# A gated decoder layer in split fp32: opening by column halves, moved low parts, loads and reductions, and last weight chunks by token halves

## The reference, cut to what matters

```
xn = rmsnorm(x, norm_mix); proj = xn @ w_in
k, v = rmsnorm(mem) @ w_k, rmsnorm(mem) @ w_v        # 256 memory rows
ya = (a_b * dwconv3(a_c * a_x)) @ w_out_a
yb = silu(layernorm(dwconv31(b_val * sigmoid(b_glu)) + bias)) @ w_out_b
yx = softmax(q @ k.T / 16) @ v @ w_out_x             # samples: cached k, v
h  = x + (sig(g0)*ya + sig(g1)*yb + sig(g2)*yx) @ w_o
h  = h + (silu(hn @ w_ff_gate) * (hn @ w_ff_up)) @ w_ff_down,  hn = rmsnorm(h)
y  = rmsnorm(h)
```

## Time and profile before

| | |
|---|---|
| median of 3 runs | 1111.93 us (1111.69 to 1114.23) |
| the profiled execution | 1113.01 us, span 1111.3 us |
| TensorE busy | 1089.8 us, 98% of the span |
| VectorE, ScalarE, GpSimd busy | 547.3, 490.6, 132.8 us |
| mean granted TensorE clock | 0.993 of full speed |
| first product of kv0, of kv1, first product of the b stage | 10.15, 18.35, 72.37 us |
| end of the last down product | 1097.6 us |
| moved by the DMA engines | 215.85 MB |

### The profile page before, as it was taken

The page is one execution under the profiler, slowest core; times in us unless marked ns, Lnnn a source line. Parts: engine busy times, 40 slices in busy tenths (PEclk is TensorE's granted clock), DMA queues, the critical chain, the costliest instruction groups (busy, mean ns, idle before and its releaser), DMA issues.

```text
span 1111.3 us, 20957 instructions
## 1 busy us (share of the span) xinstructions
PE 1089.8 (98%) x8997; PEld 1082.8 (97%) x8997; DVE 547.3 (49%) x964; ACT 490.6 (44%) x535; POOL 132.8 (12%) x118
## 2 busy tenths in 40 slices
PE   8999999999999999999999999999999999999996
PEld 7999999999999999999999999999999999999996
DVE  5775667888978564784333523343232332300122
ACT  5634343443334433443446645643444443434431
POOL 6561000002200000000000000000000000000000
PEclk9999999999999999999999999999999999999998
DMA  9857876689796777668786788787777777787863
GB/s 306 259 164 190 213 204 158 201 213 306 212 248 154 184 203 175 152 162 185 184 210 169 185 233 211 169 189 189 202 184 188 179 189 184 174 199 180 197 147 115
DMA packets 135416, 215.85 MB, mean 194 GB/s; under 512 B 4742, under 2 KB 122846, under 8 KB 124582
## 3 DMA queue, kind: packets, MB, share of 16 engines
q0 software_dynamic: 11808, 85.99, 38.8%
q1 hardware_dynamic: 98854, 106.99, 29.7%
q10 hardware_dynamic: 24688, 21.90, 6.4%
HBM read 122.34 MB, written 7.54 MB: 117 GB/s over the span
## 4 chain that ended last, share of the span: by engine, by line
PE 84%; DVE 5%; ACT 2%; DMA 2%; issue 1%; ACTq 0%; DVEq 0%
PE acc L1634 54%; PE acc L1650 27%; DVE o_acc L1291 1%; PE acc L1831 1%; DMA k_st<-in_cache_mem_k_dram 1%; DMA w_l<-w_raw 1%; PE acc L1807 1%; DVE ubyb L1128 1%; PE acc L1608 1%; ACT w_h L544 1%; DVE k_st L1202 1%; ACT w_l L547 0%; DVE sg L1439 0%; DVE yA L1342 0%; DVE ubyb L1443 0%
## 5 line engine op out<-in xcount | busy, mean ns | idle before, releaser
L1634 PE MATMUL acc<-big_h,w_h 128*128 128x260 f32 x2016 | 408.5, 284 | 1.3 <-DVE sg L1328 1.2
L1634 PE MATMUL acc<-big_l,w_h 128*128 128x260 f32 x2016 | 405.8, 283 | 0.0
L1634 PEld LDWEIGHTS acc<-big_h,w_h 128*128 128x128 f32 x2016 | 310.9, 189 | 2.0 <-DVE sg L1328 1.4
L1634 PEld LDWEIGHTS acc<-big_l,w_h 128*128 128x128 f32 x2016 | 311.3, 189 | 0.0
L544 ACT ACTIVATE w_h<-w_raw 128x1024 fp32r<-128x1024 f32 x186 | 186.2, 1050 | 179.4 <-DMA w_raw<-in_w_ff_down_dram 59.8
L1650 PE MATMUL acc<-big_h,w_l 128*128 128x260 f32 x2016 | 253.3, 282 | 1.3 <-DMA w_l<-w_raw 1.3
L1650 PEld LDWEIGHTS acc<-big_h,w_l 128*128 128x128 f32 x2016 | 246.8, 188 | 1.7 <-DMA w_l<-w_raw 1.5
L1128 DVE SCALAR_TENSOR_TENSOR ubyb<-ubyb,prm 128x512 f32<-128x512 f32 (+1 forms) x240 | 180.3, 751 | 15.6 <-DVE ubyb L1128 9.9
L528 POOL DMA_DIRECT2D w_l<-w_raw x82 | 70.0, 854 | 899.8 <-ACT w_l L547 888.5
L547 ACT ACTIVATE w_l<-w_raw 128x2048 fp32r<-128x2048 f32 x82 | 156.2, 1905 | 23.9 <-PE acc L1650 23.9
L1634 PE MATMUL acc<-hg_h,w_h 128*128 128x260 f32 x704 | 141.9, 283 | 0.0
(11 more groups left out here) (212 smaller groups left out, 762.6 us busy)
## 6 DMA issues: line engine op xcount, KB each, us to landing
w_l<-w_raw POOLq DMA_DIRECT2D x82, 1024.0 KB, 7.8
w_raw<-in_w_in_dram SPq DMA_DIRECT2D x36, 1024.0 KB, 5.2
w_raw<-in_w_ff_gate_dram SPq DMA_DIRECT2D x11, 1024.0 KB, 5.3
w_raw<-in_w_ff_up_dram SPq DMA_DIRECT2D x11, 1024.0 KB, 5.2
k_st<-in_cache_mem_k_dram ACTq DMA_DIRECT2D x8, 1024.0 KB, 8.8
v_st<-in_cache_mem_v_dram ACTq DMA_DIRECT2D x8, 1024.0 KB, 11.8
w_raw<-in_w_ff_down_dram SPq DMA_DIRECT2D x8, 1024.0 KB, 6.6
w_raw<-in_w_v_dram SPq DMA_DIRECT2D x4, 1024.0 KB, 6.7
```

Of the source, the lines that this page charges most:

```text
L1634: last = M.matmul(out[:, b, 0:HALF], w_h[:, slot, k, cols], xs[:, k_at + k, b * HALF:(b + 1) * HALF], start=start and k == 0 and xs is x[0 ...
```

## The change

Five parts, named by where they act.

1. **Opening.** Gain, high part, low part and the products of kv0 go by halves of 4 blocks, alternating between the two mem tiles, so that the products of one half run while the other is prepared. ScalarE squares the second mem tile later. The low part of weight chunk 0 is subtracted by VectorE (`first_chunk_lo`), and GpSimd starts with chunk 1 after the first root refinement. Ten filling transposes on TensorE before kv0 are gone.
2. **Low part of x one chunk on.** `prep(c)` no longer ends with `norm_lo`; that follows one chunk later. A second buffer `nrm_o` makes room.
3. **cx stage.** `group_max` comes first on VectorE, ahead of convolution steps and tile products; `sample_sum(1)` moves behind the tile work of its pass; the convolution steps are dealt out anew (same 24).
4. **xT loads** are issued after the loads of chunks ob2 and ob3 instead of ob1 and ob2.
5. **End.** The last two weight chunks are taken for tokens 0 to 259 first and then for 260 to 519; rows, squares, mean and root of the first token half (`ya`) are interleaved with the products of the second (`yb`). Chunk 93 joins `SUB`. The order of uses changes from `y2, d3, y3, ms` to `y2, ya, d3, yb`.

```diff
-WARM, FILL = 16, 10
+WARM = 16
-SUB = (*range(C_B + 2), C_CX + 2, C_CX + 4)
+SUB = (*range(C_B + 2), C_CX + 2, C_CX + 4, C_END - 1)
...
-    for name in ("d0", "d1", "y0", "d2", "y1", "y2", "d3", "y3", "ms"):
-        use(name, 1 if name == "ms" else 2)
+    for name in ("d0", "d1", "y0", "d2", "y1", "y2", "ya", "d3", "yb"):
+        use(name, 1 if name in ("ya", "yb") else 2)
...
+    nrm_b = [nrm_t, at("nrm_o", [P, KT, P], f32, o_ub + 4 * D)]
@@ SyncE, ob stage @@
-                if j in (1, 2):
-                    if j == 1:
+                if j >= 2:
+                    if j == 2:
                         sp.wait_ge(acc_done, T["gb"] + 10)
@@ GpSimd @@
+                if c == 0:
+                    continue
                 if c in SUB:
+                    if c == 1:
+                        pool.wait_ge(refined, 5)
+                    elif c == C_END - 1:
+                        pool.wait_ge(d_used, 7)
@@ ScalarE, opening @@
+            def memory_hi(m, h):
+                act.wait_ge(mem_gain, 2 * m + h + 1)
+                ks = slice(h * HK, (h + 1) * HK)
+                nc.scalar.activation(mn[0][:, ks, m * P:(m + 1) * P], (nrm_t, nrm_2)[m][:, ks, :], ACT.Copy) \
+                    .then_inc(mem_hi, 1)
-            squares(1, P)
-            norm_tile(T["mem"], mn[0], slice(0, P), P)
+            for m, h in itertools.product(range(2), range(2)):
+                memory_hi(m, h)
...
-            norm_tile(T["mem"] + 1, mn[0], slice(P, 2 * P), P, nrm_2)
+            squares(1, P)
@@ VectorE, opening @@
+            memory_gain(0, 0)
+            memory_gain(0, 1)
+            memory_gain(1, 0)
+            memory_lo(0, 0)
+            memory_gain(1, 1)
+            V.memset(mx[:, 0:1], 0.0).then_inc(acc_read, 2)
+            memory_lo(1, 0)
+            memory_lo(0, 1)
+            memory_lo(1, 1)
+            first_chunk_lo(0)
             mean_rows(0)
-            for n in range(2):
-                norm_lo(mn, slice(n * P, (n + 1) * P), P, bufs[n])
+            first_chunk_lo(1)
             refine_rows(0)
...
-                    norm_lo(xn, slice(c * P, c * P + rows), rows, nrm_t)
@@ VectorE, loop over kv chunks c @@
+                if c == 0:
+                    mean_rows(1)
                 if c == 2:
+                    norm_lo(0)
+                if c == 6:
+                    norm_lo(4)
+                if 3 <= c < 6:
+                    norm_lo(c - 2)
@@ VectorE, cx stage @@
-            C3 = ((range(0, 5), range(5, 11)), ((), range(11, 13)), (range(13, 15), range(15, 20)), (range(20, 24), ()))
+            C3 = ((range(0, 3), range(3, 7)), ((), range(7, 13)), (range(13, 15), range(15, 20)), (range(20, 24), ()))
-                    sample_sum(it)
+                    if it > 1:
+                        sample_sum(it)
+                else:
+                    group_max()
-                if it == 0:
-                    group_max()
-                if it == 0:
-                    sample_sum(0)
+                if it < 2:
+                    sample_sum(it)
@@ TensorE, kv0 @@
+                    for h, m, n in itertools.product(range(2), range(2), range(2)):
+                        pe.wait_ge(mem_lo if n else mem_hi, 2 * h + m + 1 if n else 2 * m + h + 1)
@@ TensorE, end @@
+            for low in (False, True):
+                for j in range(2):
+                    last_products(C_END - 2, j, 0, *ks[1], low)
+            for j in range(2):
+                last_products(C_END - 1, j, 0, *ks[2], False)
+            for j in range(2):
+                last_products(C_END - 1, j, 0, *ks[2], True).then_inc(d_half, 1)
+            for j in range(2):
+                last_products(C_END - 2, j, 1, *ks[1], False)
+            last_rows(T["ya"], 0, (h_half, 0))
+            last_sums(T["ya"], 0, 2, 8, 6)
+            for j in range(2):
+                last_products(C_END - 2, j, 1, *ks[1], True)
+            for j in range(2):
+                last_products(C_END - 1, j, 1, *ks[2], False)
+                last_products(C_END - 1, j, 1, *ks[2], True).then_inc(acc_done, 1)
+            last_rows(T["yb"], 2, (acc_read, T["d3"]))
+            last_sums(T["yb"], 2, 3, 10, 7)
```

More of the change, by code:

```diff
@@ new lines, in _ @@
+            dve.wait_ge(y_sq, 7)
+            last_sum(0, HALF)
+            last_rows(T["ya"], 0, slice(0, 2))
+            last_scale(0, slice(0, 2))
+            for j in range(2):
+                use = T["d3"] + j
+                done(use)
+                V.tensor_tensor(h_sb[:, 6 + j, HALF:TOK], acc[use % 4][:, 1, 0:HALF], h_sb[:, 6 + j, HALF:TOK],
+                                ALU.add).then_inc(acc_read, 1)
+            dve.wait_ge(y_sq, 9)
+            last_sum(HALF, TOK)
+            last_rows(T["yb"], 2, slice(2, 5))
@@ L1692, in _ @@
                 pe.wait_ge(row_in[n], 16)
-                flip8(T["mem"] + n, stage[n], P)
-            for n in range(FILL):
-                flip(acc[T["kv0"] % 4][:, 0, 0:P], ident[:, :])
+                flip8(T["mem"] + n, stage[n], P, halfway=mem_flip)
             def prep(c):
@@ new lines, in last_products @@
+            def last_products(c, j, b, k0, kn, low):
+                out = acc[(T["d3"] + j) % 4][:, b, 0:HALF]
+                cols, toks = slice(j * P, (j + 1) * P), slice(b * HALF, (b + 1) * HALF)
+                if b == 0 and j == 0 and low:
+                    if c in SUB:
+                        pe.wait_ge(w_sub, subtracted(c))
+                    else:
+                        pe.wait_ge(w_rest[c % 2], turn(c) * 16)
+                for k in range(kn):
+                    if b == 0 and j == 0 and not low and k % HK == 0:
+                        pe.wait_ge(w_hi, 2 * c + k // HK + 1)
+                    if low:
+                        last = M.matmul(out, w_l[:, c % 2, k, cols], mid[0][:, k0 + k, toks], start=False,
+                                        stop=c == C_END - 1 and k == kn - 1)
+                    else:
+                        for xs in mid:
+                            last = M.matmul(out, w_h[:, c % 2, k, cols], xs[:, k0 + k, toks], start=False, stop=False)
+                return last
@@ new lines, in last_rows, with last_sums @@
+            def last_rows(use, t, ready):
+                free(use)
+                for n in (6, 7):
+                    pe.wait_ge(ready[0], ready[1] + n - 5)
+                    for s in range(2):
+                        a = ((n - 6) * 2 + s) * P
+                        flip(acc[use % 4][:, 0, a:a + P], h_sb[:, n, (t + s) * P:(t + s + 1) * P])
+                    if t:
+                        flip(acc[use % 4][0:TS, 1, (n - 6) * P:(n - 5) * P], h_sb[:, n, TP:TOK])
+            def last_sums(use, t, count, squares, sums):
+                pe.wait_ge(y_hs, sums)
+                pe.wait_ge(y_sq, squares)
+                for i in range(count):
+                    rows = P if t + i < 4 else TS
+                    for n, src in enumerate((hs, sgf[:, 1, :])):
+                        last = M.matmul(acc[use % 4][0:rows, 1, 256 + i:257 + i], src[:, (t + i) * P:(t + i) * P + rows],
+                                        ones[:, 0:1], start=n == 0, stop=n == 1)
+                last.then_inc(acc_done, 1)
```

190 lines of the change are left out of this document (116 added, 74 removed).

## The result

The changed kernel takes 1106.96 us (median of 5, 1104.67 to 1107.67); the kernel before, run beside it, 1112.26 (1111.69 to 1114.23). The medians differ by 5.3 us. By the ratio over all their runs, 0.9945 with a 95% interval of 0.9932 to 0.9957, it is 6.1 us faster (4.8 to 7.6) where 10.3 were forecast, and the median is 1.5 us above the range. The profiled execution is the fastest of the five: 1104.67, span 1102.9.

A forecast was written before the change was run, and what follows sets the result against it. TensorE, busy throughout from 630 to 1097.6 us, was taken as the bound. Savings of 4.2 + 3.1 + 1.3 + 1.7 = 10.3 off 1111.93 gave 1101.6 us; likeliest 1099.5 to 1103.5, range 1098.5 to 1105.5.

The forecast's parts named there:

- The xT loads: ob stage: the later xT loads speed ob0's low-part DMA and remove TensorE's wait, saving 1.3 us, between 0 and 1.3.
- the room only at ob2: ob stage: ob2's low-part DMA, even as slow as 10.0 us, lands 3.0 us before TensorE needs it.
- the delay is moved and not removed: ob stage: by round robin xT delays whatever low-part DMA it meets, by 2.2 us, within 3.0 of room.
- The opening: Up to the b stage: VectorE comes earlier, so the b stage starts near 68.2, saving 4.2 us, between 2.0 and 5.8.
- What came back: Opening: VectorE's new waits for k,v products and ScalarE's copies, and blocked low parts, take back about 2.3 us.
- the low bound of 2.0: Opening: with all four low parts blocked by GpSimd, 2.17 us less, so only 2.0 is saved.
- The cx stage: cx stage: waits for `m_rep` and in cx4 go, 1.8 and 1.3 us, saving 3.1, between 1.5 and 3.2.
- The norm of head 0: cx stage, before cx5's second tile: late next, at 302.1 against 302.8, hidden by 0.7; a slip costs what it slips.
- The end: Last pass to the last store: products end later but stores start earlier, saving 1.7 us net, between 0.7 and 3.0.
- the wait of 1.3 for y2's first rows: Last pass: d3's second tile takes y2's accumulator before VectorE has read it, losing 1.3 us.
- What is added between the products: End: four transposes and four narrow products among TensorE's products, 0.5 + 0.4 us, 0.9 in all.
- The clock: Rival, chance 0.13: the clock falls at the opening's end, before the b stage, costing 1.5 us: 1103.1, twice 1104.6.

The follow-up runs named there:

- c4: The kernel before with only the xT loads moved (part 4 alone): 1115.11 us, ratio 1.0015.
- d1: The changed kernel with each xT half held until TensorE has ended the chunk before (ob0, ob1): 1105.18 us, ratio 0.9932.
- d2: c4 with each xT half held until TensorE has ended the chunk before (ob0, ob1): 1112.90 us, ratio 0.9992.
- a4: The changed kernel without part 4, its xT loads in their old places: 1106.47 us, ratio 0.9948.
- c3: The changed kernel with only the 928 KB convolution state copy moved, to the second down pass: 1104.70 us, ratio 0.9922.
- a3: The kernel before with part 5, the end, alone: 1111.30 us, ratio 0.9987.
- a1: The kernel before with part 3, the cx stage, alone: 1109.76 us, ratio 0.9973.
- a2: The kernel before with parts 1 and 2, the opening and the later low part of x, alone: 1111.39 us, ratio 0.9987.
- b2: The changed kernel with xT loaded in quarters behind the loads of ob2, ob3, wo0 and wo1: 1104.87 us, ratio 0.9925.
- b4: The changed kernel with squares, root and refinement of x tiles 2 to 4 put behind prep(1): 1104.14 us, ratio 0.9929.
- b1: The changed kernel timed again with no edit: 1106.42 us, ratio 0.9950.
- b3: The changed kernel with the 928 KB DRAM-to-DRAM copy of convolution state moved to the x stage: 1105.43 us, ratio 0.9936.
- c1: The changed kernel with the edits of b2 and b4 and the 928 KB copy in the second down pass: 1102.59 us, ratio 0.9909.
- c2: The changed kernel with the ten filling transposes ahead of kv0 put back: 1108.18 us, ratio 0.9948.

## Why the prediction was wrong, by its steps

- **The xT loads, forecast 1.3: the step that failed.** "ob1's DMA has a load and an xT half beside it as before" names the right companions and misses their order. The order follows from the saving itself: SyncE's next load goes out when ob0's low-part DMA has landed (landed 629.57, issued 629.59; changed, 619.61 and 619.62), and as that DMA takes 7.6 instead of 10.0, the load and the xT half behind it come sooner against ob1's. The prediction had the time of that load, 627.4, and did not lay it beside the issue of ob1's low-part DMA, 629.16. SyncE's xT half and GpSimd's low-part DMA for ob1, before and then changed:

```profile
630.00 0.58 SPq L471 DMA_DIRECT2D xT<-xt_scratch  x1
```

```profile
629.16 0.86 POOL L528 DMA_DIRECT2D w_l<-w_raw  x1 [8.75 <-ACT w_l L547]
```

```profile
620.11 0.51 SPq L478 DMA_DIRECT2D xT<-xt_scratch  x1
```

```profile
621.62 0.85 POOL L541 DMA_DIRECT2D w_l<-w_raw  x1 [8.75 <-ACT w_l L560]
```

  Before, the xT half is 0.8 behind, and the DMA takes 9.0. Changed, it is 1.5 ahead, and the DMA takes 11.7; in c4, 0.5 ahead, 13.8. The saving at ob0 came (1.4 to 1.6), and ob1 took back 1.1 to 1.4, or 4.6 to 4.8 with a clock fall. d1 and d2 show it from the other side. So part 4, forecast 1.3, is worth about nothing inside the change (a4) and -2.0 alone (c4). I had counted the room only at ob2, whose DMA took 8.1 with no wait, as forecast. From the round robin between queues (the Trainium skill, DMA: Bandwidth & Descriptors, Queues, rings and completion order) the prediction had drawn that the delay is moved and not removed. In the changed kernel the trace agrees, at ob1: 1.59 gained, 1.41 lost. In d1 it does not: 1.60 gained and nothing lost.
- **The wait in `wo` and feed-forward, forecast none.** -1.29 and -0.98 in the two profiles: a term that the prediction put at nothing without a reason. It goes when the 928 KB copy is elsewhere (c3) and when the xT halves are held (d1). a4 and a3 have it with xT in its old place, before, a1 and a2 do not: the stream is near its limit there, and what tips it stays open beyond these two handles. One part can be read from the traces: the low-part DMA of the last `wo` chunk took 14.9, 14.0, 13.8 and 13.0 when issued 0, 0.5, 0.8 and 2.2 us behind the copy (a4, b2, b4, b1), 11.2 and 10.9 at 3.9 and 4.0 (d1, a2), and 8.8 at 6.5 (changed) and 6.6 (before). Open too is the 0.3 to 0.5 that each kernel with the new opening loses "to gb" (b3 loses 1.2 more to its copy), of which a wait of 0.2 for `merged` is all that the waits show.
- **The opening, forecast 4.2: mis-sized.** kv1's start was right: 16.75 for 16.9. Behind it I expected 2.75 and got 1.6. The waits for the high copies went as forecast, 5.3 before and 0.4 after. What came back was put at 2.3 and was more. Two of VectorE's waits from the start of kv1 to that of the b stage, of the changed kernel, and then the first of them in before, where the second is missing:

```profile
DVE kv_f L1125 <- PE acc L1831: 3.8, 3, 1.9
...
DVE st L1014 <- ACT junk_norm L601: 2.4, 2, 1.8
```

```profile
DVE kv_f L1077 <- PE acc L1733: 2.0, 1, 2.0
```

  The 2.4 for ScalarE's squares, behind a late load, stood in no term: I had VectorE waiting for products and copies only. b4 gives back some 0.6 of it. The waits for products grew by 1.8. The blocked low parts are not the reason: 1.69, 2.26, 2.31 and 3.27 us make 9.5, where before has 3.40, 1.23, 3.38 and 1.23, 9.2, and VectorE is busy for 40.95 us of that stretch where it was 41.08. The Trainium skill (GPSIMD Engine Reference, Key points) had each of them open to this; the trace agrees in that all four were slowed, by 0.5 to 2.0 us against 1.23. It does not bear out the low bound of 2.0 that the prediction drew for that case: the opening gave 3.2. Without b3's fall at 41 us, and without b4, c1 and c2, which alter the opening, seven profiles of the new opening give 2.3 to 4.0, mean 3.1; the first mem rows landing early or late (waits of 0.6 to 2.2) are part of that spread.
- **The cx stage, forecast 3.1: right.** 3.15 or 3.16 in eleven kernels, timed alone 3.1. The norm of head 0 did not slip.
- **The end, forecast 1.7: near in size, 1.89, by two errors that nearly cancel, which is luck.** From last product to end 9.87, forecast 9.8. But the wait of 1.3 for y2's first rows did not come. VectorE's read ends at 1070.89, 7.1 us behind the last product of the pass before; in a1, a2, c4 and d2, with the same end, it is 4.8 behind. The load of chunk 92 was late in that one execution. In the other four ScalarE copies the chunk after a wait for TensorE and not for the DMA:

```profile
1064.23 2.01 ACT L544 ACTIVATE w_h<-w_raw 128x1024 fp32r<-128x1024 f32 x2 [7.08 <-DMA w_raw<-in_w_ff_down_dram]
```

```profile
1063.10 2.01 ACT L544 ACTIVATE w_h<-w_raw 128x1024 fp32r<-128x1024 f32 x2 [3.86 <-PE acc L1634]
```

  The first line is of before, the second of c4. Without that wait, my sum gives 3.0, and the end has 1.89. What is added between the products is not 0.9 but 1.9 (35.65 us for 33.79 from the second-last pass's end to the last product). The chain shows 1.5 of that: turns and narrow products of the first token half, and 64 products in 7.95 instead of 7.66.

```profile
1059.74 7.95 PE acc L1728 x64
...
1085.47 0.44 PE acc L1700 x4
1085.90 0.79 PE acc L2088 x8
```

- **The clock.** That it falls at a new place was a rival at 0.13; it fell at kv0 in four of eleven profiles with the new opening, each time behind late mem rows, and the missing transposes are not needed for it (d2 has them and falls, ahead of them). It did not fall ahead of the b stage, where I had looked for it. The argument against, that waits of 1.7, 1.3 and 1.2 had no fall behind them, rested on one trace: the wait for `m_rep`, of the same length, has one behind it in c4 and d2, and the wait of 1.70 for `nrm_o` in b3 and c2.

Timed, the parts alone give 3.1, 1.5, 1.6 and -2.0 by their medians, together 4.2; the whole gives 5.3 and, in b1, 6.4. With the intervals of the four, some 2.5 us on their sum, the times do not show that the parts fail to add. The table does show it in one place: at ob1 part 4 alone loses 4.77 with a clock fall, within the whole 1.41 and 1.36 without one. There the xT half is 0.5 ahead of the low-part DMA in the one and 1.5 in the other.

## What to carry to other kernels

When a transfer is moved, write down for each DMA it will meet who is issued first, to the half microsecond, and not only who is in flight beside it: at ob1 one 1040 KB transfer 0.8 us behind cost nothing, 0.5 us ahead it cost a wait of 3 us and a clock fall. Behind is not free either: at ob0, where there is less room, the same transfer 1.1 us behind cost the 1.3 us that this part set out to save. Before taking a wait from a single profile as a rule of the kernel, ask what made it late; if that was one load, another execution may not have it. And for effects near 1 us, compare stage ends of several profiles. Single runs of one kernel here lie 1 to 10 us apart and its medians up to 0.9, while the cx stage's gain agrees to 0.01 us in eleven kernels and the end's to 0.1.

## What the runs showed of the hardware

A low-part DMA of 1 MB took 6.9 to 15.2 us over the sixteen profiles, the longest with the 928 KB copy issued within 0.3 us of it (15.2 in b3, 14.9 in a4). With 1040 KB of xT beside it, it took 13.8 (0.5 us ahead, c4), 11.7 (1.5 ahead) and 9.0 (0.8 behind), and at ob0 10.0 (1.1 behind) against 7.6 and 8.6 with none.

The granted clock drops to the 1.2 GHz level for about two slices of 2 us, at a cost of 1.5 us where TensorE is the bound. At 8 us it follows each wait for the first rows of 1.6 and more and none of 1.4 and less. Later the same wait is followed by a fall in one execution and by none in another: the 2.0 for `kv_f` has one in before, a1 and d2 and none in a3 and c4; the 1.6 to 1.7 for `nrm_o` in two of nine; the 1.6 to 1.7 for `m_rep` in c4 and d2 and not in before, a2 and a3. It also follows the DMA waits of 3.0, 2.8 and 1.8 (c4, c2, a2) and one of a4's two of 1.8, but not the other. And in five of sixteen profiles it comes between 333 and 343 us behind 20 narrow products, with no gap of TensorE.
